# The inverse root of three norms spread by a round trip through HBM, not by a diagonal and two matmuls

## What is computed

```python
def rmsnorm(x, g):
    inv = lax.rsqrt(jnp.mean(x * x, axis=-1, keepdims=True) + RMS_EPS)
    return (x * inv) * g

def reference(x, p, ...):
    h = x
    for i in range(2):
        hn = rmsnorm(h, mix_norm_g[i])
        mix = diff_attention(hn, ...) if i == 0 else multiscale_pool(hn, ...)
        h = h + mix
        h = h + conv_glu_ffn(rmsnorm(h, ffn_norm_g[i]), w_up[i], conv_w[i], conv_b[i], w_down[i])
        gate = sigmoid(rmsnorm(h, ple_norm_g[i]) @ w_ple_gate[i])
        h = h + gate * (p[i] @ w_ple_proj[i])
    return rmsnorm(h, final_norm_g)
```

## Time and profile before

| | us |
|---|---|
| median of 3 runs | 1103.35 (1103.12 to 1103.98) |
| the profiled execution, its own time | 1103.46 |
| span of its trace | 1101.7 |
| TensorE busy | 1089.8 (99%) |
| VectorE busy | 719.2 (65%) |
| ScalarE busy | 515.0 (47%) |
| GpSimd busy | 25.2 (2%) |
| granted TensorE clock, mean | 0.998 |

### The profile page before, as it was taken

One profiled execution on the slowest core, in us unless ns is written; L12 is line 12 of the kernel. 1 busy time (PEld: TensorE's weight loads), 2 busy tenths in 40 slices (PEclk: granted clock), 3 DMA queues, 4 the chain that ended last, 5 costly groups with the idle time before them and its releaser, 6 DMA issues.

```text
span 1101.7 us, 14447 instructions
## 1 busy us (share of the span) xinstructions
PE 1089.8 (99%) x5152; PEld 908.5 (82%) x5152; DVE 719.2 (65%) x1107; ACT 515.0 (47%) x775; POOL 25.2 (2%) x82
## 2 busy tenths in 40 slices
PE   9999999999999999999999999999999999999997
PEld 8878888888888888888888888888888888888886
DVE  7567878575775377743776778777437773477636
ACT  6456667364643144421445677444314442244554
POOL 0001110020000000000000000000000000000001
PEclk9999999999999999999999999999999999999999
DMA  8213243233233233232233222233322233233411
GB/s 330 62 58 83 62 96 79 65 109 103 92 99 115 77 95 95 96 115 79 95 103 127 95 94 77 77 95 99 114 78 101 95 106 115 77 95 95 134 58 76
DMA packets 31295, 107.88 MB, mean 98 GB/s; under 512 B 3600, under 2 KB 3600, under 8 KB 31248
## 3 DMA queue, kind: packets, MB, share of 16 engines
q1 hardware_dynamic: 30288, 105.13, 30.8%
q0 software_dynamic: 672, 1.59, 0.6%
q10 hardware_dynamic: 288, 0.53, 0.2%
HBM read 105.12 MB, written 2.11 MB: 97 GB/s over the span
## 4 chain that ended last, share of the span: by engine, by line
PE 93%; DVE 4%; ACT 2%; issue 1%; POOL 0%; DVEq 0%; ACTq 0%; POOLq 0%
PE bank L1257 29%; PE bank L1259 29%; PE bank L1258 29%; PE bank L1351 1%; PE bank L1277 1%; DVE w_lo L821 1%; PE bank L1364 1%; DVE probs L943 1%; DVE h_tok L1209 1%; DVE c L1207 0%; ACT probs L494 0%; DVE emb L1220 0%; PE bank L1318 0%; ACT w_hi L392 0%; PE bank L1544 0%
## 5 line engine op out<-in xcount | busy, mean ns | idle before, releaser
L1257 PE MATMUL bank<-x_hi,w_hi 128*128 128x512 f32 x896 | 350.2, 391 | 0.0
L1259 PE MATMUL bank<-x_hi,w_lo 128*128 128x512 f32 x896 | 348.8, 389 | 0.0
L1258 PE MATMUL bank<-x_lo,w_hi 128*128 128x512 f32 x896 | 348.7, 389 | 0.0
L821 DVE TENSOR_TENSOR w_lo<-w_raw,w_hi 128x1024 fp32r<-128x1024 f32 (+1 forms) x189 | 226.0, 1197 | 52.6 <-ACT w_hi L392 52.5
L392 ACT ACTIVATE w_hi<-w_raw 128x1024 fp32r<-128x1024 f32 (+1 forms) x189 | 193.8, 1031 | 109.4 <-PE bank L1259 109.4
L1259 PEld LDWEIGHTS bank<-x_hi,w_lo 128*128 128x128 f32 x896 | 168.2, 188 | 35.0
L1257 PEld LDWEIGHTS bank<-x_hi,w_hi 128*128 128x128 f32 x896 | 168.2, 188 | 34.8 <-issue 0.4
L1258 PEld LDWEIGHTS bank<-x_lo,w_hi 128*128 128x128 f32 x896 | 168.3, 188 | 34.5
L1257 PE MATMUL bank<-g_hi,w_hi 128*128 128x512 f32 x352 | 136.9, 389 | 0.0
L1258 PE MATMUL bank<-g_lo,w_hi 128*128 128x512 f32 x352 | 136.9, 389 | 0.0
L1259 PE MATMUL bank<-g_hi,w_lo 128*128 128x512 f32 x352 | 136.9, 389 | 0.0
(11 more groups left out here) (218 smaller groups left out, 1172.7 us busy)
## 6 DMA issues: line engine op xcount, KB each, us to landing
w_raw<-in_weights SPq DMA_DIRECT2D x189, 512.0 KB, 3.5
gain_and_h<-in_xT SPq DMA_DIRECT2D x7, 256.0 KB, 5.6
o_inv<-o_rows POOLq DMA_DIRECT2D x6, 256.0 KB, 4.8
out<-emb SPq DMA_DIRECT2D x3, 512.0 KB, 3.0
p_raw<-in_pT SPq DMA_DIRECT2D x1, 1024.0 KB, 10.0
w_raw<-in_weights SPq DMA_DIRECT2D x2, 256.0 KB, 3.7
gain_b<-in_final_gain SPq DMA_DIRECT2D x1, 512.0 KB, 4.0
gain_and_h<-in_gain_and_x ACTq DMA_DIRECT2D x1, 260.0 KB, 3.6
```

Of the source, the lines that this page charges most:

```text
L821: dve.tensor_tensor(w_lo[s][:, 0:w], w_raw[s][:, 0:w], w_hi[s][:, 0:w].bitcast(F32), ALU.subtract).then_inc(lo_done, 1)
L1257: pe.matmul(dst, w1, m1, start=start and i == 0, stop=False)
L1258: pe.matmul(dst, w1, m0, start=False, stop=False)
L1259: last = pe.matmul(dst, w0, m1, start=False, stop=stop and i == len(parts) - 1)
```

## The change

Three of the four spread rows are no longer made by a diagonal and two matmuls. In their place GpSimd runs `norm_row`: it waits for the column (`icol_done`), writes it to HBM (2 KB), waits for the write, and reads the row back into 128 partitions (256 KB). VectorE runs `inverse_row`: it waits for the read (`row_landed`) and copies the row to `inv`, in the order of the tokens. The first mixing norm lands in `o_inv`, which the attention uses later; the other two in a new tile, `ffn_row`. ScalarE's copy, VectorE's three operations and TensorE's two matmuls go away at these norms. The first layer's embedding norm (`NORM_PLE0`) stays as it was. The core of the diff:

```diff
+        ffn_row = sb("ffn_row", [P, SEQ], F32, ffn)
+        inv_row = [o_inv, ffn_row, ffn_row]
...
-        spread_of = {NORM_MIX0: 1, NORM_FFN0: 2, NORM_PLE0: 3, NORM_FFN1: 4}
+        row_of = {NORM_MIX0: 0, NORM_FFN0: 1, NORM_FFN1: 2}
+        spread_of = {NORM_PLE0: 1}
+        norm_inverses = {NORM_MIX0: 1, NORM_FFN0: 2, NORM_PLE0: 3, NORM_FFN1: 4}
...
-            inverse(NORM_MIX0)
             split_hi(8)
...
-            inverse(NORM_FFN0)
             for layer in range(DEPTH):
...
                     split_hi(PHASES["emb1b"][0] + 1 + LOOK)
-                    inverse(NORM_FFN1)
...
+            def norm_row(norm):
+
+                r = row_of[norm]
+                pool.wait_ge(icol_done, norm + 1)
+                pool.dma_start(inv_rows[r].rearrange("(p t) -> p t", t=TT), icol).then_inc(row_written, 16)
+                pool.wait_ge(row_written, 16 * (r + 1))
+                pool.dma_start(inv_row[r][:, :], inv_rows[r:r + 1, :].broadcast_to((P, SEQ))).then_inc(row_landed, 16)
+
+            norm_row(NORM_MIX0)
+            pool.wait_ge(inv_done, 1)
             for hp in range(ROW_HEADS):
...
             pool.wait_ge(evac_done, result_of("wo", KT - 1))
+            norm_row(NORM_FFN0)
             for g, win in enumerate(POOL_WINDOWS):
...
+            norm_row(NORM_FFN1)
             for t in range(TT - 1):
...
+            def inverse_row(norm):
+
+                r = row_of[norm]
+                dve.wait_ge(row_landed, 16 * (r + 1))
+                dve.tensor_copy(inv[:, :].rearrange("p (t c) -> p t c", t=TT),
+                                inv_row[r][:, :].rearrange("p (c t) -> p t c", t=TT)).then_inc(inv_done, 1)
+                dve.wait_ge(inv_done, norm_inverses[norm])
...
                 if hd == 0:
-                    dve.wait_ge(inv_done, 1)
+                    inverse_row(NORM_MIX0)
...
-            dve.wait_ge(inv_done, spread_of[NORM_FFN0])
+            inverse_row(NORM_FFN0)
...
-                    dve.wait_ge(inv_done, spread_of[NORM_FFN1])
+                    inverse_row(NORM_FFN1)
...
-                if k == 1:
-                    pe.wait_ge(diag_done, 1)
-                    pe.wait_ge(vlo_done, 1)
-                    spread(bank[0]).then_inc(spread_done, 1)
...
-            norm_spread(NORM_FFN0)
...
-                                def ready_and_spread():
-                                    norm_spread(norm)
-                                    ready()
```

More of the change, by code:

```diff
@@ L46 @@
 BAND = P + EDGE
+N_ROWS = 3
 def plan():
@@ L94, in result_of, with hybrid_trunk @@
     return RESULTS_BEFORE[name] + u + 1
-def hybrid_trunk(nc, gain_and_x0, xT, pT, weights, final_gain, columns, out, o_rows):
+def hybrid_trunk(nc, gain_and_x0, xT, pT, weights, final_gain, columns, out, o_rows, inv_rows):
     with ExitStack() as ctx:
@@ L242, in hybrid_trunk @@
         table_loaded = sem("table_loaded")
+        row_written, row_landed = sem("row_written"), sem("row_landed")
         CH = 2 * FT
@@ L399, in inverse @@
                 act.wait_ge(spread_done, spread_of[norm])
-                act.activation(inv[:, :], bank[7 if norm else 0][:, :], ACT.Copy, scale=float(D_MODEL)).then_inc(inv_done, 1)
+                act.activation(inv[:, :], bank[7][:, :], ACT.Copy, scale=float(D_MODEL)).then_inc(inv_done, 1)
             act.dma_start(gain_and_h[:, 0:KT + SEQ], gain_and_x0[:, :]).then_inc(x_in[0], 16)
@@ L1170, in _ @@
                 split_lo(PHASES[name][0] + LOOK + 2)
-                dve.wait_ge(inv_done, spread_of[norm])
+                dve.wait_ge(inv_done, norm_inverses[norm])
                 def next_input(m):
@@ L1403, in queries @@
                     if hd == 0:
-                        pe.wait_ge(inv_done, 1)
+                        pe.wait_ge(vlo_done, 1)
                     if hd == 1:
@@ L1571, in up_body @@
                             parts = x_parts(slot_of(PHASES[name][0] + u), KT * norm + 1 if first and u == 0 else None)
-                            if first and u == 1 and layer:
-                                weights, moving, ready = parts[KT // 2]
-                                def ready_and_spread():
-                                    norm_spread(norm)
-                                    ready()
-                                parts[KT // 2] = (weights, moving, ready_and_spread)
                             unit(name, u, a, parts)
@@ L1741 @@
     o_rows = nc.dram_tensor("o_rows", (ROW_HEADS, SEQ), F32, kind="Internal").ap()
-    hybrid_trunk(nc, *args, result, o_rows)
+    inv_rows = nc.dram_tensor("inv_rows", (N_ROWS, SEQ), F32, kind="Internal").ap()
+    hybrid_trunk(nc, *args, result, o_rows, inv_rows)
     r = run_bass_kernel_spmd(nc, [arrays], core_ids=[0])
```

## The result

| | before | after |
|---|---|---|
| median, 9 runs each, one chip | 1103.40 us (1103.02 to 1104.22) | 1106.54 us (1105.10 to 1108.14) |
| profiled execution, its own time | 1103.46 | 1107.06 |
| span of its trace | 1101.7 | 1105.3 |
| granted TensorE clock, mean | 0.998 | 0.996 |

The ratio is 1.0027, with a 95% interval of 1.0017 to 1.0036. The change makes the kernel slower by about 3 us. The forecast was 1105.5, with a range of 1103.2 to 1108.0. The spread of the runs is part of the result. Before, nine runs lie within 1.2 us. After, three runs stand at 1105.10, 1105.27 and 1105.42, all with a mean clock of 0.998. The other six stand between 1106.47 and 1108.14, with clocks of 0.995 to 0.997.

What follows compares the result with a forecast made beforehand. TensorE, busy for 99% of the span, was taken as the bound. Terms of -0.46 at A, -0.80 at B and +3.44 at C sum to +2.18 us on 1103.35, giving 1105.5 us, range 1103.2 to 1108.0.

Steps and rivals of the forecast that it cites:

- Removed matmuls: The pair of spreading matmuls at each of three places takes 0.46 us of TensorE's stream; together 1.38 us.
- A: First mixing norm, near 34 us: the row's longer path is free, so the place gives -0.46 us.
- C: Second layer's feed-forward norm, near 694 us: the row comes late, +3.9 - 0.46 = +3.44 us.
- B: First layer's feed-forward norm, near 247 us: the path is free, -0.46 - 0.34 = -0.80 us.
- The tables' effect: At B, GpSimd's band tables move behind the row and stop slowing VectorE's low part of `wo`: 0.34 us back.
- the first cover: At B, 3 us spare between the usable row at 250.3 and the evacuation just ahead of 254.07.
- the second cover: At B, another 3.4 us between the weight split's end at 255.29 and TensorE's use at 258.71.
- C, the path: Reciprocal to usable row 7.85 us: hop 0.2, write 2.0, read 4.8, hop 0.05, copy 0.8; evacuation 0.16 later.
- C, the stall: Evacuation 4.44 us late delays the fourth unit's low part; TensorE loses 3.9 us, and the next unit has 0.3 margin.
- The clock: Rival: the stall at C drops TensorE's clock to half speed, 2 us more, 1107.5 us; chance 13%.
- No second unit stalled: Rival: the late chain reaches a second unit at C, or B's cover fails, 1107 us; chance 5%.
- the row was not in time at C: Rival: the row is in time at C too, so the three places give -1.72, 1101.6 us; chance 7%.

Runs made afterwards that it cites:

- the best version: Kernel after, splits of four units made ahead of VectorE's wait at C, and C's two DMAs issued from ScalarE's queue: 1101.57 us, ratio 0.9982.
- the kernel that keeps C's pair: Kernel after with C put back to the diagonal and two matmuls, rows by DMA at A and B only; measured again: 1102.04 us, ratio 0.9988.
- the kernel before with only that edit: Kernel before with GpSimd waiting for the feed-forward norm's column at B ahead of its band tables, no rows: 1103.05 us, ratio 0.9997.
- the kernel with the filler: Kernel after with 14 matmuls of 512 columns that nobody reads, ahead of the fourth unit at C: 1105.37 us, ratio 1.0017.
- three units ahead: Kernel after with high and low weight splits of three units, not one, made ahead of the wait for the row at C: 1103.74 us, ratio 1.0001.
- ScalarE's queue: Kernel after with C's two DMAs issued by ScalarE instead of GpSimd: 1104.73 us, ratio 1.0014.
- second write: Kernel after with GpSimd writing C's row twice before reading it: 1110.74 us, ratio 1.0064.

## Why the prediction was right, and where its sizes were off

**Removed matmuls: right.** 0.46 a pair. At A TensorE is ahead by 0.45 (62.79 against 63.24), and the best version's median is 0.47 below that of the kernel that keeps C's pair.

**B: right, with less cover than I gave it.** TensorE is 1.36 us ahead at C's sums, where I had 1.26. The tables' effect was real (0.34 forecast; 0.41 by TensorE's sums in the kernel before with only that edit). But I priced the write at 2.0 us, from one head's rows, and it took 4.0, behind a weight load issued at 241.44. The row was usable at 251.6, not at 241.55 + 7.85 = 249.4, and the first cover was 0.4 us, not some 3. The six writes of the attention stage took 2.0 to 2.3 us. In all nine traces with a row at B a load is issued 0.65 us ahead of the write, and the write took 3.8 to 4.2. So the price of the earlier trace rows did not carry to this stretch. No run moves the load away, so that the load is the cause is likely, not shown. The error cost nothing, since the second cover held, and that was luck as far as the write goes.

**C, the path: right.** Forecast 8.01 us from the reciprocal's end to the evacuation, measured 690.28 to 698.38 = 8.10. Inside it, the hop took 0.31 and not 0.2, the round trip of the write 1.99 (2.0), the read 5.0 (4.8), and the copy 0.62 and not 0.80. The sum of a stride's surcharge and a plain copy (0.42 + 0.38) was too dear.

**C, the stall: right.** Forecast 3.9 us of TensorE's stream, measured 3.8. The next unit did not stall: its low part ended at 709.72, and TensorE asked for it at 704.41 + 3.46 + 16 x 0.227 = 711.50. Of this margin of 1.8 us the slow clock gave 1.64, so without it about 0.15 would have been left, of the 0.3 forecast.

**The clock: the term that was mis-sized.** The forecast left it out as a rival, with 13% and 2 us, and named a clock that drops at C as a sign of being wrong. That sign is in the profiled run: the granted clock falls during the stall, and the matmuls resume 0.43 us apart. It shows in six of the nine runs by their mean clock and time, and those six make the median. The forecast fits the other three (1105.1 to 1105.4), and the kernel with the filler (1105.37). The sum missed the median by 1.0 us, and this is where. The price was near (1.64 us in the profiled run; the six lie 1.2 to 2.9 us above the middle one of the three). The chance was not, nor the condition. The rival asked for a stall of a little over 4 us, since in one row the clock fell about 4 us behind the last matmul. The runs show that these 4 us are no bound. The clock fell 3.6 us behind the last matmul's end in the kernel after and 2.1 us behind it with the row at C only, and with three units ahead it fell although TensorE had waited for 1.79 us only. Even by that one row, two durations that are equal within their errors speak for a chance near one half, not one in eight, and then the two microseconds belong beside the forecast as an equal case.

**The other rivals.** No second unit stalled, B's covers held, the row was not in time at C, and the read there was not quick (5.0 us).

**Open.** What decides whether the clock falls in a given run is not shown. Waiting for 3.05 and 6.6 us cost it in every run seen. Waiting for 3.65 us cost it in six of nine. With ScalarE's queue, where the profiled run waited for 2.2 us, it was lost in five of eleven, by their times and mean clocks. In the kernel with three units ahead, 1.8 us of waiting cost it in the profiled run (1105.34) and, by their times (1103.2 to 1104.0), in none of the ten others. The waits are those of the one profiled run of each kernel.

## What to carry to other kernels

A wait that is long on a side engine is priced by what is queued behind it on that engine. Before moving a producer to a slower path, either put the work that the bottleneck needs next ahead of the wait, and far enough ahead for the late chain to catch up, or leave it where it is. A stall of TensorE of a few microseconds costs more than its length, because the matmuls behind it may run at half rate. So forecast it with the clock's loss as a likely part, and check the spread of the runs, not only their median.

## What the runs showed of the hardware

- The clock's loss is not proportional to the stall. The stretches at the lower level lasted 3.4 us (after), 6.8 us (row at C only), 6.8 us (second write, behind a wait of 6.6) and 3.4 us (three units ahead, profiled run). In that last run TensorE had waited only 1.79 us, and the first matmuls behind the wait still started 0.34 and 0.23 apart, until about 714.2:

```profile
713.00:714.00 1.00, 0.49 (x2) 0.46 (x3) 1.00 (x2) 0.00 (x0) 0.00 (x0) 1.00 0.00 0
714.00:715.00 1.00, 1.00 (x4) 0.75 (x4) 0.86 (x3) 0.00 (x0) 0.00 (x0) 0.59 0.12 29
...
717.00:718.00 1.00, 1.00 (x5) 0.82 (x4) 1.00 (x3) 0.38 (x2) 0.00 (x0) 0.71 0.00 0
```

- Fourteen useless matmuls in the stall kept the clock at 1.00, and the median was 1.2 us lower.
- A write of 2 KB from 128 partitions, issued by GpSimd, took 2.0 to 2.3 us from its issue to that of the read where no load was issued just ahead of it, and 3.8 to 4.6 us where a weight load was. By ScalarE's queue it took 1.45 us at C. A read of 256 KB into 128 partitions landed in 3.5 to 3.9 us at A, where the next weight load was issued 2.2 us behind it, and in 3.4 to 5.7 at B and C in all kernels. The Trainium skill, page "DMA: Bandwidth & Descriptors", section "Anatomy of one DMA — SWDGE (gpsimd) path", fits a DMA's time, and by that fit the estimate for this read is 2.6 us. No run came under 3.4 us.
- A copy of 128x512 fp32 with a stride of four elements takes 0.61 to 0.64 us, against 0.42 without. A two-input product with that stride costs 1.07 against 0.69. The surcharge is about 0.2 for the one and 0.38 for the other.
